# A transformer block on one core: the last sixth of the adaLN product moved into the expert V pass, and the query weight loaded k tile by k tile

## The reference, cut to what matters

```python
mod = silu(c) @ ada_w + ada_b                    # c: 2048; ada_w: 2048 x 12288
shift1, scale1, gate1, shift2, scale2, gate2 = split(mod, 6)
h = rms_norm(x, pre_mix_g) * (1 + scale1) + shift1
y = mixer(h)                                     # w_in, pooling and attention, w_out
x = x + gate1 * rms_norm(y, post_mix_g)
h = rms_norm(x, pre_ffn_g) * (1 + scale2) + shift2
q = h @ w_q                                      # w_q: 2048 x 2048
# scores against sub_keys, top 16 of 2 x 128, best 16 of 256 pairs, softmax -> gate per (token, expert)
y = (gelu(h @ U.T) * gate) @ V                   # U, V: 16384 x 2048, only picked experts have gate != 0
x = x + gate2 * rms_norm(y, post_ffn_g)
```

## Time and profile before

| | us |
|---|---|
| median of 3 runs | 2152.22 (2151.8 to 2155.94) |
| the profiled execution's own time | 2155.08 |
| its span in the trace | 2152.3 |
| PE busy | 1946.9 (90%) |
| PE weight loads busy | 1757.5 (82%) |
| DVE busy | 1520.1 (71%) |
| ACT busy | 898.1 (42%) |
| POOL busy | 432.6 (20%) |

### The profile page before, as it was taken

One profiled execution on the slowest core, in us unless ns is written; L12 is line 12 of the kernel. 1 busy time (PEld: TensorE's weight loads), 2 busy tenths in 40 slices (PEclk: granted clock), 3 DMA queues, 4 the chain that ended last, 5 costly groups with the idle time before them and its releaser, 6 DMA issues.

```text
span 2152.3 us, 37807 instructions
## 1 busy us (share of the span) xinstructions
PE 1946.9 (90%) x12388; PEld 1757.5 (82%) x12388; DVE 1520.1 (71%) x2136; ACT 898.1 (42%) x1311; POOL 432.6 (20%) x290
## 2 busy tenths in 40 slices
PE   0489989798999999999999997679999999999995
PEld 0479658698999999999999997568888888888884
DVE  6897489775689999999976667975555555555554
ACT  1143233453334444444444445654444444444443
POOL 1000020000234444444444446840000000000001
PEclk9799859899999999999999999999999999999998
DMA  9989469979567676666677771045555555555553
GB/s 392 414 306 353 157 246 367 295 227 268 131 168 183 180 184 182 180 182 176 175 186 180 184 183 59 0 134 192 192 194 195 194 190 192 194 195 192 190 193 117
DMA packets 227889, 436.99 MB, mean 203 GB/s; under 512 B 23106, under 2 KB 157696, under 8 KB 214016
## 3 DMA queue, kind: packets, MB, share of 16 engines
q1 hardware_dynamic: 226240, 427.84, 63.9%
q0 software_dynamic: 1536, 8.48, 1.0%
q10 hardware_dynamic: 64, 0.02, 0.0%
HBM read 432.04 MB, written 4.21 MB: 203 GB/s over the span
## 4 chain that ended last, share of the span: by engine, by line
PE 79%; DVE 10%; DMA 3%; issue 3%; ACT 2%; DVEq 1%; SPq 1%; POOL 0%; ACTq 0%; POOLq 0%
PE ps L591 14%; PE ps L592 14%; PE ps L593 14%; PE ps L877 11%; PE ps L878 11%; PE ps L880 11%; DVE acc L1229 3%; DVE hotB L1636 2%; DMA ring<-in_ada_w_dram 2%; PE ps L586 2%; DMA i<-consts_dram 1%; DVEq L1636 1%; DVE ring_low L1237 1%; PE ps L568 1%; PE ps L703 1%
## 5 line engine op out<-in xcount | busy, mean ns | idle before, releaser
L591 PE MATMUL ps<-h2H,eH 128*128 128x256 f32 x2048 | 581.5, 284 | 5.8 <-DVE eL L1584 4.5
L592 PE MATMUL ps<-h2L,eH 128*128 128x256 f32 x2048 | 581.0, 284 | 0.0
L593 PE MATMUL ps<-h2H,eL 128*128 128x256 f32 x2048 | 580.9, 284 | 0.0
L1667 DVE TENSOR_TENSOR eL<-raw,eH 128x1024 fp32r<-128x1024 f32 x256 | 313.6, 1225 | 338.2 <-ACT eH L1175 338.2
L1175 ACT CAST eH<-raw 128x1024 fp32r<-128x1024 f32 x256 | 269.9, 1055 | 385.4 <-PE ps L880 379.8
L496 POOL TENSOR_TENSOR eL<-raw,eH 128x1024 fp32r<-128x1024 f32 x128 | 311.4, 2433 | 572.9 <-ACT eH L1101 572.9
L877 PE MATMUL ps<-eH,aH 128*128 128x512 f32 x1024 | 399.2, 390 | 3.6 <-DVE eL L1667 3.6
L591 PEld LDWEIGHTS ps<-h2H,eH 128*128 128x128 f32 x2048 | 394.6, 193 | 6.7 <-DVE eL L1584 5.2
L878 PE MATMUL ps<-eL,aH 128*128 128x512 f32 x1024 | 398.9, 390 | 0.0
L593 PEld LDWEIGHTS ps<-h2H,eL 128*128 128x128 f32 x2048 | 394.7, 193 | 0.0
L592 PEld LDWEIGHTS ps<-h2L,eH 128*128 128x128 f32 x2048 | 394.6, 193 | 0.0
(11 more groups left out here) (254 smaller groups left out, 2313.1 us busy)
## 6 DMA issues: line engine op xcount, KB each, us to landing
raw<-in_peer_u_dram SPq DMA_DIRECT2D x1024, 128.0 KB, 3.0
raw<-in_peer_v_dram SPq DMA_DIRECT2D x256, 512.0 KB, 3.4
ring<-in_ada_w_dram SPq DMA_DIRECT2D x48, 2048.0 KB, 19.9
ring<-in_w_out_dram SPq DMA_DIRECT2D x8, 2048.0 KB, 11.9
ring<-in_peer_wq_dram SPq DMA_DIRECT2D x32, 512.0 KB, 15.5
ring<-in_w_in_dram SPq DMA_DIRECT2D x6, 2048.0 KB, 14.7
ring<-in_w_uq_dram SPq DMA_DIRECT2D x2, 1536.0 KB, 9.0
ring<-in_w_in_dram SPq DMA_DIRECT2D x2, 1280.0 KB, 11.7
```

Source lines behind the costliest of these rows:

```text
L591: pe.matmul(o, lh, rh, start=start, stop=False, skip_group_check=True)
L592: pe.matmul(o, lh, rl, start=False, stop=False, skip_group_check=True)
L593: return pe.matmul(o, ll, rh, start=False, stop=stop, skip_group_check=True)
L1667: dve.tensor_tensor(eL[:, slot, :], raw[:, slot, :], eH[:, slot, :].bitcast(F32), ALU.subtract).then_inc(v_lo, 1)
```

## The change

Part 6 of the adaLN product leaves the query stage.

- The load list has only the eight w_q blocks and the keys at its end. Each w_q block is loaded in eight transfers of one k tile each, over all 128 partitions (256 KB), in place of four transfers of 32 partitions.
- The `ada(1)` after each pair in the query stage, `ada_columns(5, 3)`, `gate_column(1, ...)`, `gate_rows(1, 3)` and `gate_out(1, 3)` are gone, and so are the waits of ACT on them. Two of the small vector loads at the start are gone too.
- In the V pass DVE has one step (`last_gate`) after each of the tiles 3 to 34. The weight comes in 16 pieces of 1 MB (8 KB for each partition) through three buffers in space that the U pass has left; SP loads the first three after the U pass, POOL loads the others when the second step on the piece three before is done.
- After tile 35 DVE block-transposes the 128 x 2048 sums and after tile 38 reduces them by 32. POOL gathers the four quarters with four small transfers, adds them on 32 partitions, stores the row to `gate_dram` by single elements, loads it back as a row on all partitions, and loads the bias and the gain as rows. DVE adds the one after tile 89 and multiplies the other after tile 104.
- POOL's load of x1 for the tail stands behind the pieces and the sums.

```diff
-        per_slot[n % SLOTS] += 64 if key[0] == "wq" else 16
+        per_slot[n % SLOTS] += 128 if key[0] == "wq" else 16
-            + between + mixed(wout, 4) + mixed(wq, 5) + [("keys", 0, 0)])
+            + between + mixed(wout, 4) + wq + [("keys", 0, 0)])
...
-                    for q in range(4):
-                        sp.dma_start(wide(kind, i, 8 * h)[q * QUAD:(q + 1) * QUAD],
-                                     wq_v[q, :, ks, i * W:(i + 1) * W]).then_inc(done, 16)
+                    for k in range(8):
+                        sp.dma_start(wide(kind, i, 8 * h)[:, k, :],
+                                     wq_v[8 * h + k, :, :, i * W:(i + 1) * W]).then_inc(done, 16)
...
+            sp.wait_ge(u_used, 2 * TILES)
+            for k in range(3):
+                load_piece(sp, k)
             for j in range(RING, 6):
                 load_v(j // 2, j % 2, j, j % RING)
...
-            pool.wait_ge(row_stored, 32)
+            for k in range(3, KT):
+                pool.wait_ge(piece_step, 2 * (k - 2))
+                load_piece(pool, k)
+            pool.wait_ge(quarter_ready, 1)
+            for q in range(4):
+                pool.dma_start(quarters[0:QUAD, q, :], quarter[q * QUAD:(q + 1) * QUAD, :]).then_inc(quarters_in, 16)
...
+            pool.dma_start(gate_dram[1].rearrange("(b l) -> l b", l=QUAD), half2[0:QUAD, 2, :],
+                           allow_slow_non_contiguous=True).then_inc(row2_stored, 16)
...
-            ada_columns(5, 3)
             for i in range(ROUND):
                 u_tile(0, i, i < 3)
-            gate_rows(1, 3)
...
                 if j == 7:
-                    act.wait_ge(acc_used, 12)
+                    act.wait_ge(acc_used, 10)
...
             u_round(0, first=True)
-            gate_out(1, 3)
...
                     if n or j >= 2:
                         weight_low("wq", n, j)
-                    ada(1)
...
-            gate_column(1, 5, 3, V_B5, V_PO2)
...
-            with dve.Fori(1, TILES // 3) as r:
+            def last_gate(step):
+                k, h = step // 2, step % 2
+                if h == 0:
+                    dve.wait_ge(*piece_done(k))
+                a, w = (t[:, h * 1024:(h + 1) * 1024] for t in (sums2, piece[k % 3]))
+                if k == 0:
+                    dve.tensor_scalar(a, w, c_act[:, 0:1], None, ALU.mult).then_inc(piece_step, 1)
+                else:
+                    dve.wait_ge(piece_step, step - 1)
+                    dve.scalar_tensor_tensor(a, w, c_act[:, k:k + 1], a, ALU.mult, ALU.add).then_inc(piece_step, 1)
...
+            for tile in range(3, 36):
+                v_tile(tile, tile % 3, False)
+                if tile < 35:
+                    last_gate(tile - 3)
+            dve.wait_ge(piece_step, 2 * KT)
+            dve.transpose(sums2[:], sums2[:]).then_inc(sums_turned, 1)
+            for tile in range(36, 39):
+                v_tile(tile, tile % 3, False)
+            dve.wait_ge(sums_turned, 1)
+            dve.tensor_reduce(quarter[:], sums2[:].rearrange("p (b l) -> p b l", l=QUAD), AX_X,
+                              ALU.add).then_inc(quarter_ready, 1)
```

More of the change, by code:

```diff
@@ L60 @@
 V_B2 = P
-V_B5 = V_B2 + KT
-V_PO1 = V_B5 + KT
-V_PO2 = V_PO1 + KT
-V_ALL = V_PO2 + KT
+V_PO1 = V_B2 + KT
+V_ALL = V_PO1 + KT
 TWO_PI_A = 6.28125
@@ L209, in hybrid_block @@
     gate2 = at("gate2", M + 4096, [D])
+    piece = [at(f"piece{i}", M + 2048 * i, [D]) for i in range(3)]
+    sums2 = at("sums2", M + 6144, [D])
+    quarter = at("quarter", S + 1712, [KT * 4])
+    quarters = at("quarters", M + 6144, [4, KT * 4])
+    half2 = at("half2", M + 6400, [3, KT * 4])
+    extra = at("extra", M + 6144, [D])
     raw = at("raw", M + 8192, [RAW, HF])
@@ L271, in hybrid_block @@
         y2_sq, y2_rc, y2_rs, tail_in = sem("y2_sq"), sem("y2_rc"), sem("y2_rs"), sem("tail_in")
+        piece_first = [sem(f"piece_first{i}") for i in range(3)]
+        piece_in = [sem(f"piece_in{i}") for i in range(3)]
+        piece_step, sums_turned, quarter_ready, quarters_in, half_chain = (
+            sem("piece_step"), sem("sums_turned"), sem("quarter_ready"), sem("quarters_in"), sem("half_chain"))
+        row2_stored, gate2_in, extra_in, gate2_ready = (
+            sem("row2_stored"), sem("gate2_in"), sem("extra_in"), sem("gate2_ready"))
         scaled_ready, out_stored = sem("scaled_ready"), sem("out_stored")
@@ L351, in add_x1, with piece_done, load_piece @@
                               ALU.add).then_inc(out_ready[tt], 1)
+        def piece_done(k):
+            return (piece_first[k], 16) if k < 3 else (piece_in[k % 3], 16 * (k // 3))
+        def load_piece(eng, k):
+            eng.dma_start(piece[k % 3][:], ada_v[:, k, 5 * D:6 * D]).then_inc(piece_done(k)[0], 16)
         ada_v = ada_w[0].rearrange("(p k) n -> p k n", k=KT)
@@ L468, in _ @@
             pool.dma_start(quad_rows(V_B4), quads(ada_b[0, 4 * D:5 * D])).then_inc(vrow_in, 16)
-            for m, v in enumerate((ada_b[0, 2 * D:3 * D], ada_b[0, 5 * D:6 * D], post_mix_g[0], post_ffn_g[0])):
+            for m, v in enumerate((ada_b[0, 2 * D:3 * D], post_mix_g[0])):
                 pool.dma_start(vrow2[m * KT:(m + 1) * KT, :], rows(v)).then_inc(vrow_in, 16)
@@ L548, in transpose_vectors @@
                 pe.wait_ge(cst_in, 16)
-                pe.wait_ge(vrow_in, 208)
+                pe.wait_ge(vrow_in, 176)
                 pe.transpose(ps[:, 1, 0:P], vrow[:, :], ident).then_inc(vec_t, 1)
-                pe.transpose(ps[:, 1, P:P + 64], vrow2[0:64, :], ident[0:64, 0:64]).then_inc(vec_t, 1)
+                pe.transpose(ps[:, 1, P:P + 2 * KT], vrow2[0:2 * KT, :], ident[0:2 * KT, 0:2 * KT]).then_inc(vec_t, 1)
             def ada_columns(i, bank):
@@ L1671, in _, with gate_row @@
                 v_tile(j, j, True)
-            with dve.Fori(1, TILES // 3) as r:
+            def last_gate(step):
[8 more added lines that the diff above has]
+                    dve.scalar_tensor_tensor(a, w, c_act[:, k:k + 1], a, ALU.mult, ALU.add).then_inc(piece_step, 1)
+            def gate_row(i, op):
+                dve.wait_ge(gate2_in, 16)
+                dve.wait_ge(extra_in, 16 * (i + 1))
+                dve.tensor_tensor(gate2[:], gate2[:], extra[:], op).then_inc(gate2_ready, 1)
+            for tile in range(3, 36):
[9 more added lines that the diff above has]
+                              ALU.add).then_inc(quarter_ready, 1)
+            with dve.Fori(13, 30) as r:
+                for j in range(3):
+                    v_tile(r * 3 + j, j, False)
+            gate_row(0, ALU.add)
+            with dve.Fori(30, 35) as r:
+                for j in range(3):
+                    v_tile(r * 3 + j, j, False)
+            gate_row(1, ALU.mult)
+            with dve.Fori(35, TILES // 3) as r:
                 for j in range(3):
@@ L1676, in _ @@
                 v_tile(TILES - 2 + j, j, False)
-            dve.wait_ge(tail_in, 32)
+            dve.wait_ge(tail_in, 16)
+            dve.wait_ge(gate2_ready, 2)
             dve.wait_ge(y2_sq, 1)
```

20 lines of the change are left out of this document (15 added, 5 removed).

## The result

The changed kernel takes 2186.75 us (median of 4 runs, 2183.89 to 2188.1) against 2152.01 for the kernel before in the same job: a ratio of 1.0157, 95% interval 1.0139 to 1.0175. The forecast was 2129.1. So it is 34.7 us slower where 23 us less were forecast, and outside the range. The profiled execution of after took 2186.57 us, with a span of 2184.8.

A forecast was written before the change was run, and what follows sets the result against it. PE was taken as the bound in the U and V passes, while the query stage waited for DVE and the DMA engines. Gains of 14.6 + 8.5 + 0 = 23.1 us from 2152.2 gave 2129.1 us, range 2123 to 2141.

The forecast's parts named there:

- The query stage: Query stage without adaLN steps and their 16 MB of loads: 14.6 us shorter, low end 12.9, high end 17.2.
- it could cut the landing or double it, and neither reaches PE: Query stage: the new w_q transfer shape costs PE nothing, with 30 us of cover against a longest landing of 28.7.
- six of the eight blocks are now asked for [...] before 415 us: Query stage: SP issues six w_q blocks early; the seventh waits until about 451 us and is needed about 510.
- a block that lands 59 us after its issue: Query stage: how late a w_q block would have to land to change the forecast sum.
- the 1 MB rule: w_q loads: a transfer should be 1 MB or more, which spoke against cutting 512 KB to 256 KB.
- a halved clock behind pair 2: Query stage: PE's 2.3 us wait may or may not halve the clock; booked as one slow stretch, 2.6 us.
- The start of the U pass: Start and round 0 of the U pass, without `ada_columns` and the later hole: 8.5 us gained, low end 5.
- Rival 3: V pass: the adaLN step on DVE delays low parts and reaches PE; in full 41 us, 2170; chance 0.05.
- rival 1: V pass: V loads beside the adaLN weight pieces land late, 4 to 15 us, giving 2133 to 2144; chance 0.12.
- POOL's x1 load moves behind all this, to about tile 40: V pass: the x1 load is issued later, still 490 us before the tail; no cost booked.
- the nearest row: Start of V pass: 3 MB of x1 and gate2 under way, landings at most 6.7 us, no PE wait; zero cost.
- I take zero: V pass: the store of the row by single elements costs between nothing and 3 us; booked at zero.

The follow-up runs named there:

- experiment 1: The changed kernel with w_q loaded as before, four transfers of 32 partitions and 512 KB per block; 2133.54 us, 0.9907 of the kernel before.
- experiment 3: The changed kernel with each w_q k tile read as 128 neighbouring rows, still 256 KB transfers (another product than the reference); 2138.19 us.
- experiment 4: The changed kernel with each w_q k-tile transfer cut into four of 32 partitions, 64 KB each; 2133.81 us.
- experiment 5: The changed kernel with each w_q k tile cut into two transfers of 64 partitions, 128 KB each; 2349.48 us.
- experiment 7: Old-shape w_q loads and gate row stored in 128-byte runs, plus bias row behind tile 72 and x1 in four 512 KB loads from tile 104; 2129.51 us.
- experiment 6: Three runs on old-shape w_q loads: x1 held to V tile 60, 2135.29 us; gate row stored in 128-byte runs, 2133.37; both, x1 behind tile 75, 2133.61.

## Why the prediction was wrong, step by step

**The query stage, and the step that failed.** The step is the price of the new w_q transfer, booked at nothing with "it could cut the landing or double it, and neither reaches PE". I compared the landing time of one transfer with the cover of one block. But this stage is bound by how fast the blocks follow one another, not by how late one lands: experiment 1 has landings of 17.5 us and no wait to speak of, after has issues of 2.46 us and 36.3 us of waits. With it went "six of the eight blocks are now asked for [...] before 415 us": SP issues the sixth block at 420 us in experiment 1, and at 491 in after. The bound that I gave, a block that lands 59 us after its issue, was the wrong quantity. The right one stands in the diff: the source is read as `k q l n` with k fixed, so its slowest dimension is q, which is 4. On four engines a block of 2 MB takes 8 x 2.46 = 20 us against 11.4 us of PE, and eight blocks 8 x 20 = 160 us, which is the 163 that SP's row shows. No row of before had that shape. So the range should have had a low-rate end, and it had none. The transfer's price was 53 us (experiment 1), where nothing was booked.

Experiments 3, 4 and 5 vary that dimension and the rest separately: 128, 32, 4 and 2 outermost rows give 0.43, 0.42, 2.46 and 2.46 us for an issue of 256, 64, 256 and 128 KB.

The Trainium skill states this (DMA: Bandwidth & Descriptors, Why a DMA increments its semaphore by 16 and not by 1): the number of engines is the largest number up to 16 that divides the slowest dimension that isn't 1, of both access patterns. By this rule, 4 and 2 engines; the trace agrees, with shares of 0.27 (4.3 engines) and 0.13 (2.1), and with four and two packets under way. In the prediction I weighed two other rules of the Trainium skill against the trace, the ports of a 32-partition transfer, which spoke for the change, and the 1 MB rule, which spoke against it. Experiments 3 and 4 show that neither decides here: 256 KB and 64 KB transfers, to 128 and to 32 partitions, all kept PE fed.

**The rest of the query stage** was right. With transfers that use all the engines it takes 95.3 to 97.7 us, against 98.6 with a halved clock behind pair 2 and 96.0 without. The one wait for `ring_low` was forecast at 2.3 us, and is 2.4 in experiment 7 and 1.6 in experiment 1. No other wait for a low part is left, and the clock is 1.00 from 460 us on.

**The start of the U pass: right.** From the keys' transposes to the first U matmul 12.3 us in experiments 1 and 7, where 14.6 less 2.25 = 12.35 was forecast, and PE waits there 1.1 us (1.3 forecast). In after:

```profile
594.81 0.39 PE L631 MATMUL ps<-h2H,eH 128*128 128x256 f32 x1 [1.09 <-DVE eL L1619]
...
595.00:630.00 35.00, 34.99 (x291) 34.79 (x291) 33.30 (x74) 15.76 (x19) 16.13 (x7) 1.00 0.70 186
```

The clock is 1.00 in round 0, and behind it there is no hole as in the earlier trace rows and no halved clock as in the earlier trace rows. DVE is at 33.30 of 35.00 us, so what was named as late next, came close but did not reach PE. The stage from the first U matmul to the first V matmul is 6.6 us shorter (5.9 in experiment 1), where 6.3 were booked.

**The V pass: the steps right, the loads mis-sized.** Rival 3, the step that reaches PE, did not come: 240 matmuls in 54 us are 4.4 a us, and 443 in 100 us are the same, with DVE at 73% where "about 75%" was said. Nor did the first part of rival 1, the pieces: V loads land in 4.7 us at the median beside them instead of 3.2, below the 8 us that were worked out as covered, and PE does not wait. (The sign that was named for this rival, ACT waiting for `in_peer_v`, does show there, 22.9 us in 9 waits from 1500 to 1600, but none of it reaches PE.) Wrong is "POOL's x1 load moves behind all this, to about tile 40" at no price, and the store "I take zero". I looked at each of the late loads alone, and took the start of the V pass, where 3 MB of them cost nothing, as the nearest row. That row did not carry over: in the middle of the pass, with 4 MB and the element store together, a V load took 14.1 us to land, beyond the 8.7 that were worked out as covered, and PE stopped. The measured price is 7.8 us in after and 7.5 in experiment 1 (705.3 less 697.8). Without the single elements 4.4 are left (702.2), which is the burst of 4 MB. The elements add 3.1 to it when they stand beside the burst, and without x1 beside them PE waits 0.6 us. So the term "between nothing and 3 us" held their size; the burst had no term. Nor had the halved clock behind the hole.

**The sum.** With both errors out, which is experiment 7, the steps nearly add up: 24.0 us of span less than before (2152.3 less 2128.3), where 23.1 were forecast, and 2129.5 us where 2129.1 were. That the last two agree to 0.4 us is luck. The query stage gained 17.1 us instead of 14.6, since the clock was not halved behind pair 2 in that trace (the forecast's own high end was 17.2), the end lost 1.7 that no term had, and the six executions of this kernel spread over 5.2 us. So the prediction was right, within a few us, on what the move of the adaLN part is worth, and wrong on the two things that came along with it.

**What stays open.** From the start of the last V matmul to the end the changed kernel and all that derive from it take 23.7 to 23.9 us, the kernel before 22.2. The rows up to the issue of the last store are equal in length, so the 1.5 us lie behind it, and no row shows what they are. The shares of the hole do not add up: the single elements cost little without x1 (0.6 us of waits), the burst without the elements 3.3, both together 5.2 and a halved clock. Why a V load beside the elements lands so late is not shown; the rows show only the 60 GB/s and the landings. And each V pass length rests on one trace.

## What to carry to other kernels

Before you price a transfer by its bytes, write down the slowest dimension of its source as it is issued: with 4 or 2 there, the transfers of this case ran on 4 and 2 DMA engines, and a reshape that made them "wider" made each block take 20 us, where 32 rows outermost and four times as many transfers took 13.4. Price a stream of loads by its rate against what it feeds (us for a block against us of PE for it), and only a single load by its landing time. And where loads are moved beside a stream that must not stop, list them together with the instant at which each is issued: here 21 MB cost nothing in experiment 7, all but the first three pieces in portions of 1 MB or less, 4 MB at once cost 4.4 us (702.2 less 697.8) and 3 MB at once 1.2 to 1.8 us of waits.

## What the runs showed of the hardware that I had not expected

- One DMA engine moved 25.5 GB/s (102 / 4 and 51 / 2), with 84 ns for a packet of 2 KB. Issues on SP's queue came no faster than the few engines took the bytes: every 2.46 us for 256 KB on four engines and for 128 KB on two, against 0.43 us in experiment 3. So slow transfers held up all that stood behind them in SP's queue, the keys and U loads too (issued from 554 us on, in experiment 3 from 474).
- A store of 2048 single elements, 8 KB in all, landed in 10.2 us (9.6 without x1 beside it), and from 1676 to 1680 us the engines moved 60 GB/s at a share of 0.65. In runs of 128 bytes the same row landed in 3.1 us.
- The granted clock behind a wait isn't a function of the wait alone. Behind pair 2's wait of 2.42 us the clock was 0.55 for 3 us (the run with x1 later, in experiment 6), behind one of 2.41 us it stayed at 1.00 (experiment 7). The forecast's "it may or may not be" is all that these runs support:

```profile
446.00:449.00 3.00, 2.87 (x14) 2.90 (x15) 3.00 (x3) 1.57 (x2) 0.00 (x0) 0.55 1.07 212
```
```profile
446.00:449.00 3.00, 3.00 (x27) 3.00 (x27) 3.00 (x3) 1.33 (x3) 0.00 (x0) 1.00 1.08 215
```
